# The mixer of a two-block transformer kernel turned round: q, k and v chunks last, linear attention and gating threaded through them, z tiles between the pairs, output products in two halves, head norms by token

## The reference

```
x = norm(ALPHA x + swiglu_half(x, w1, w3, w2))            # d_ff 2816
proj = x @ w_in                                            # 1024 -> u, v, qkv, z, beta, decay, cq, ck, cv, r, low
a = spatial_gating(u, v)                                   # mixes tokens in chunks of 128
b = gated_deltanet(silu(conv4(qkv)), z, beta, decay)       # 8 heads, chunks of 64, triangular solve, 8 steps
c = gla(cq, ck, cv, r, low)                                # 4 heads, linear attention in chunks of 64
x = norm(ALPHA x + [a b c] @ w_out)
x = norm(ALPHA x + swiglu_half(x, w1, w3, w2))
```

## Time and profile before

| what | us |
|---|---|
| median of three runs | 3182.92 |
| lowest and highest | 3181.77, 3183.39 |
| the profiled execution | 3187.82 |
| its span, first to last instruction | 3185.7 |
| PE busy | 2966.3 |
| DVE, ACT, POOL busy | 1318.6, 1110.5, 818.0 |

### The profile page before, as it was taken

One profiled execution on the slowest core, in us unless ns is written; L12 is line 12 of the kernel. 1 busy time (PEld: TensorE's weight loads), 2 busy tenths in 40 slices (PEclk: granted clock), 3 DMA queues, 4 the chain that ended last, 5 costly groups with the idle time before them and its releaser, 6 DMA issues.

```text
span 3185.7 us, 46789 instructions
## 1 busy us (share of the span) xinstructions
PE 2966.3 (93%) x19136; PEld 2399.5 (75%) x19136; DVE 1318.6 (41%) x1507; ACT 1110.5 (35%) x1290; POOL 818.0 (26%) x288
## 2 busy tenths in 40 slices
PE   7999999889999999988799999999999978899997
PEld 5776677658788887768678888788877858678886
DVE  3534444343223235636552323422157454643215
ACT  4334434422233325532233323333236421233323
POOL 4112211230101263334001135011443432000144
PEclk9999999979999999989999999999999989899998
DMA  4111111112222332210022233222332200122233
GB/s 167 40 60 53 43 45 46 53 53 93 94 92 92 111 140 88 93 54 1 15 79 93 92 119 135 81 104 92 125 126 84 84 28 1 41 80 95 103 125 113
DMA packets 36094, 257.50 MB, mean 81 GB/s; under 512 B 4032, under 2 KB 4080, under 8 KB 5872
## 3 DMA queue, kind: packets, MB, share of 16 engines
q1 hardware_dynamic: 34416, 249.65, 21.7%
q0 software_dynamic: 1536, 5.83, 0.6%
HBM read 253.30 MB, written 2.16 MB: 80 GB/s over the span
## 4 chain that ended last, share of the span: by engine, by line
PE 72%; issue 12%; DVE 6%; POOL 5%; ACT 3%; DMA 0%; ACTq 0%; DVEq 0%; POOLq 0%; SPq 0%
PE ps L2056 42%; PE ps L1572 6%; PE ps L1527 5%; PE ps L1564 4%; POOL wl L1194 4%; PE ps L2169 3%; PE ps L1627 2%; PE ps L1616 2%; PE ps L885 1%; ACT wh L1771 1%; PE ps L1582 1%; DVE wl L1882 1%; PE ps L1657 1%; DVE sqa L1915 1%; PE ps L2135 1%
## 5 line engine op out<-in xcount | busy, mean ns | idle before, releaser
L1194 POOL TENSOR_TENSOR wl<-raw,wh 128x2048 fp32r<-128x2048 f32 x114 | 525.2, 4607 | 817.7 <-ACT wh L1771 817.7
L2056 PE MATMUL ps<-xh,wh 128*128 128x512 f32 x1680 | 664.0, 395 | 20.7 <-DVE qkv L648 11.0
L2056 PE MATMUL ps<-xl,wh 128*128 128x512 f32 x1680 | 658.2, 392 | 0.0
L2056 PE MATMUL ps<-xh,wl 128*128 128x512 f32 x1680 | 658.0, 392 | 0.0
L1771 ACT ACTIVATE wh<-raw 128x2048 fp32r<-128x2048 f32 x224 | 427.5, 1908 | 408.1 <-PE ps L2056 351.9
L1882 DVE TENSOR_TENSOR wl<-raw,wh 128x2048 fp32r<-128x2048 f32 x112 | 285.7, 2551 | 578.8 <-ACT wh L1771 557.0
L2056 PEld LDWEIGHTS ps<-xh,wh 128*128 128x128 f32 x1680 | 317.7, 189 | 92.6 <-issue 14.7
L2056 PEld LDWEIGHTS ps<-xl,wh 128*128 128x128 f32 x1680 | 318.0, 189 | 67.8 <-issue 2.4
L2056 PEld LDWEIGHTS ps<-xh,wl 128*128 128x128 f32 x1680 | 317.8, 189 | 66.7
L1736 POOL TENSOR_TENSOR hl<-hf,hh 128x1024 f32 x44 | 105.8, 2404 | 980.8 <-ACT hh L1781 980.8
L2056 PE MATMUL ps<-hh,wh 128*128 128x512 f32 x704 | 277.1, 394 | 1.6 <-POOL wl L1194 1.2
(11 more groups left out here) (361 smaller groups left out, 4663.1 us busy)
## 6 DMA issues: line engine op xcount, KB each, us to landing
raw<-stream SPq DMA_DIRECT2D x232, 1024.0 KB, 4.8
btw<-bias_rows POOLq DMA_DIRECT2D x2, 1536.0 KB, 8.9
x<-x_in SPq DMA_DIRECT2D x1, 2048.0 KB, 8.2
out<-x SPq DMA_DIRECT2D x4, 512.0 KB, 2.6
sgp<-sg POOLq DMA_DIRECT2D x2, 640.0 KB, 4.0
cst<-consts SPq DMA_DIRECT2D x1, 1092.0 KB, 12.2
c<-bias_consts SPq DMA_DIRECT2D x1, 1024.0 KB, 15.7
bt<-bias_rows POOLq DMA_DIRECT2D x2, 512.0 KB, 9.2
```

Source lines behind the costliest of these rows:

```text
L1194: nc.gpsimd.tensor_tensor(wl[:, p, :], raw[:, p, :], wh[:, p, :].bitcast(F32), ALU.subtract).then_inc(s["chunk_lo"], 1)
L2056: mm = te.matmul(dst, wslice(w, k), r(k), start=(start and m == 0), stop=(stop and m == len(steps) - 1))
```

## The change

The input chunks come in another order: cq and ck, u, rows, cv, v, r, then the six of q, k and v, then the two of z. The chunks from q on are computed in quarters (`chunk_q`), and behind each quarter `between` puts small products: the decay columns behind the second quarter of chunk 6, the scores of the linear attention in chunk 7, its keys by token and the spatial gating in chunk 8, its states in chunk 9, its outputs in chunk 10. The four tiles of z stand one each between the pairs of the delta rule.

A head norm is now by token: four products with two columns give each token's mean squares (`norm_columns`, L542), ACT's root and DVE's reciprocal are taken of 16 or 32 columns, and eight products of 64x128 spread the result over the features (`norm_spread`, L551), which DVE multiplies from PSUM (L573). Squares stay on ACT.

The factors on keys and values move from DVE to POOL, by pairs, between the masks of the levels. Copies by token are by pairs too, and on ACT. The products that apply the inverse are emptied pair by pair, by ACT and DVE. Of the output, each tile's product is cut in two halves of four input tiles (0, 1, 6, 7 are known before the recurrence); the first halves of six tiles come ahead of any second half, and the last head norm stands between them. The weights of the output are stored in that order. Four products of 128x128 (`busy`) stand ahead of the wait before each layer norm and twelve behind it; nobody reads their result.

```diff
+OUT_K = ((0, 1, 6, 7), (2, 3, 4, 5))
+OUT_HALVES = ((0, 0), (0, 1), (0, 2), (0, 3), (0, 4), (0, 5), (1, 0), (1, 1), (1, 2), (1, 3), (0, 6), (0, 7), (1, 4), (1, 5), (1, 6), (1, 7))
+OUT_BANK = (4, 5, 6, 7, 0, 3, 1, 2)
...
+        IN_CQK, IN_AU, IN_ROWS, IN_CV, IN_AV, IN_CR, IN_QKV, IN_Z = 0, 1, 2, 3, 4, 5, 6, 12
...
+        def norm_columns(l, pe, g, tiles, bank, src):
+
+            for t in range(tiles):
+                pe.wait_ge(s["head_square"], l * NORMED + 2 * g + t + 1)
+                for m in range(4):
+                    c = 16 * g + 8 * t + 2 * m
+                    mm = nc.tensor.matmul(ps[:, bank, c:c + 2], tmp[:, src + t, m * P:(m + 1) * P], head_mean2, start=True, stop=True)
+            mm.then_inc(s["head_ms"], 1)
...
+        def norm_spread(l, pe, g, t, bank):
+
+            pe.wait_ge(s["head_rstd"], l * GROUPS + g + 1)
+            for m in range(4):
+                for b in range(2):
+                    c = 16 * g + 8 * t + 2 * m + b
+                    mm = nc.tensor.matmul(ps[64 * b:64 * b + 64, bank, m * P:(m + 1) * P], ncol[:, 1, c:c + 1].to_broadcast([P, 64]), C("ident"), start=True, stop=True)
+            mm.then_inc(s["head_spread"], 1)
...
+            if 0 <= g < 4 and q == 1:
+                norm_columns(l, pe, g, 2, 5, 4)
...
+            if at == (11, 2):
+                norm_columns(l, pe, 4, 2, 5, 4)
+            if 0 <= g < 4 and q in (3, 4):
+                t = q - 3
+                if g or t:
+                    pe.wait_ge(s["head_normed"], l * NORMED + 2 * g + t)
+                norm_spread(l, pe, g, t, 4)
...
+                    chunk_q(l, OFF_IN, j, j % 2, lambda q: between(l, pe, j, q))
+                between(l, pe, j, 4)
...
-        def heads_norm_pe(pe, n_tiles, n0, first=False):
-            for t in range(n_tiles):
-                n = n0 + t
-                pe.wait_ge(s["head_square"], n + 1)
-                if not first:
-                    pe.wait_ge(s["head_std"], n - 1)
-                nc.tensor.matmul(ps[:, 6 + t % 2, :], C("head_mean"), tmp[:, t % 2, :], start=True, stop=True).then_inc(s["head_ms"], 1)
...
-                nc.vector.reciprocal(tmp[:, 4 + t % 2, :], tmp[:, 2 + t % 2, :]).then_inc(s["head_rstd"], 1)
-                dve.wait_ge(s["head_rstd"], n + 1)
-                nc.vector.scalar_tensor_tensor(out=tiles[t], in0=tiles[t], scalar=factors[t], in1=tmp[:, 4 + t % 2, :],
-                                               op0=ALU.mult, op1=ALU.mult).then_inc(s["head_normed"], 1)
...
+            def z_tile(j, t):
+                if t == 0:
+                    pe.wait_ge(evac[j % 2], n_evac(l, j % 2, OFF_IN) + j // 2)
+                chunk_q(l, OFF_IN, j, j % 2, lambda q: between(l, pe, j, q), tiles=(t,))
+            z_tile(IN_Z, 0)
+            pair(0)
+            z_tile(IN_Z, 1)
+            pair(1)
+            pe.wait_ge(evac[1], n_evac(l, 1, OFF_IN) + IN_Z // 2)
+            turned(0)
+            z_tile(IN_Z + 1, 0)
+            pair(2)
...
+            for pr, ready in ((0, (s["pair_act"], l * 8 + 7)), (1, (s["pair_dve"], d0 + 3 * PAIR_DVE + 5)), (2, (s["pair_dve"], d0 + 3 * PAIR_DVE + 6)), (3, (s["pair_dve"], d0 + 3 * PAIR_DVE + 7))):
+                pe.wait_ge(*ready)
+                pe.sem_inc(s["apart_pe"], 1)
+                by_token(kT, pr, K_BANK[pr])
+            pe.wait_ge(s["by_token_sb"], l * 8 + 2)
+            turned(3)
...
+                if pr == 3:
+                    mix_rest(l, pool, ((0, au[:, 0, :]), (1, au[:, 1, :]), (6, cr[:, 0, :]), (7, cr[:, 1, :])), 0)
...
+            for lev in range(PAIRS):
+                masks(lev)
+                if lev == 0:
+                    pool.wait_ge(s["by_token_sb"], l * 8 + 8)
+                    pool.wait_ge(s["factor_dve"], l * 2 + 2)
+                    pool.wait_ge(s["factor_act"], l * 3 + 3)
+                gp.tensor_tensor(bk[:, lev], kN[:, lev], by_token(bgN, lev), ALU.mult).then_inc(s["factored"], 1)
+                gp.tensor_tensor(vN[:, lev], vN[:, lev], by_token(bN, lev), ALU.mult).then_inc(s["factored"], 1)
+                pool.wait_ge(s["factored"], l * 3 * PAIRS + 3 * lev + 2)
+                gp.tensor_tensor(kN[:, lev], kN[:, lev], by_token(kdN, lev), ALU.mult).then_inc(s["factored"], 1)
+            masks(PAIRS)
+            for j in (IN_Z, IN_Z + 1):
+                rest(pool, c_no(l, OFF_IN) + j + 2, j % 2)
...
-            ve.tensor_tensor(bk[:, :, :, :], kN[:, :, :, :], by_token(bgN), ALU.mult).then_inc(s["factor_dve"], 1)
-            dve.wait_ge(s["factor_act"], l * 3 + 3)
-            dve.wait_ge(s["factor_dve"], k0 + 3)
-            ve.tensor_tensor(kN[:, :, :, :], kN[:, :, :, :], by_token(kdN), ALU.mult).then_inc(s["factor_dve"], 1)
...
+                add_tiles((s["out_tile"], l * 3 + 2), 4, 1, s["out_early_x"])
+                dve.wait_ge(s["out_early_x"], l * 2 + 1)
+                add_sum(l, 1, 4, 6)
+                add_tiles((s["out_tile"], l * 3 + 2), 5, 1, evac[1])
+                dve.wait_ge(evac[1], n_evac(l, 1, OFF_OUT) + 1)
+                add_sum(l, 1, 5, 7)
...
+                rest_chunk(n_out + OUTP, 0)
+                add_tiles((s["out_tile"], l * 3 + 3), 6, 1, s["out_early_x"])
+                dve.wait_ge(s["out_early_x"], l * 2 + 2)
+                add_sum(l, 1, 6, 8)
+                add_squares(l, 1, (4, 5, 6))
...
+                    for kk in ks:
+                        k = OUT_K[h][kk]
+                        if n == OUT_HALVES.index((1, 0)):
+                            pe.wait_ge(s["mixed_lo"], l * 8 + 4 + kk + 1)
+                        c = 512 * i + P * kk
+                        for a, (w, r) in enumerate(((wh, xh), (wh, xl), (wl, xh))):
+                            mm = te.matmul(ps[:, OUT_BANK[t], :], w[:, m % 2, c:c + P], r[:, k, :], start=(h == 0 and kk == 0 and a == 0), stop=(h == 1 and kk == 3 and a == 2))
...
+                for n in (0, 1):
+                    out_half(n)
+                norm_columns(l, pe, 5, 4, 2, 1)
+                out_half(2)
+                for pr in range(PAIRS):
+                    if pr:
+                        pe.wait_ge(s["head_normed"], l * NORMED + 10 + pr)
+                    norm_spread(l, pe, 5, pr, 1)
...
+                out_half(11, (0, 1))
+                shift(l, 1)
+                out_half(11, (2, 3))
+                for n in (12, 13, 14):
+                    out_half(n)
+                out_half(15, (0, 1))
+                sums(l, 1)
+                out_half(15, (2, 3))
+                busy(4)
...
+            def busy(n):
+
+                for _ in range(n):
+                    te.matmul(shift_ps[:, 0:P], C("ident"), C("feat_mean"), start=True, stop=True)
```

743 lines of the change are left out of this document (412 added, 331 removed).

## The result

| | before | after | forecast |
|---|---|---|---|
| median, us (4 runs each) | 3183.15 (3181.77 to 3185.72) | 3128.85 (3125.57 to 3133.7) | 3113 (3082 to 3148) |
| ratio, 95% interval | | 0.983 (0.9813 to 0.9847) | |
| profiled execution, us (its span) | 3187.8 (3185.7) | 3125.6 (3123.7) | 3118.5 |

The account below looks back on a forecast made before the run. TensorE bounds the kernel by its work, idle gaps and half clock. Terms -24.8, -26.5, -5.4, -6.0 and -6.6 sum to -69.3 us: 3118.5 from the profiled 3187.8, median 3113; 8-in-10 range 3082 to 3148.

Parts of the forecast that it names:

- the likeliest case: Whole kernel: the sum of terms holds within its parts, 3098 to 3130 us; chance 0.52.
- the output stage: Recurrence to layer norm: 64.7 us instead of 67.7, -3.0 a layer, with a new wait and one clock drop.
- gap in chunk 11: Linear attention's sums by token wait for ACT's late squares: TensorE idles 1.9 us a layer.
- gap ahead of level one: End of the pairs: POOL's low parts and masks come late, together 3.6 us a layer.
- levels to end of recurrence, change: Copy of u becomes four operations, only the last, 0.7 us, exposed: -2.7 us a layer; POOL's factors cost nothing.
- wait at the sums: Output stage, before the sums of squares: DVE's list is late, TensorE waits about 6 us a layer.
- the pairs' broadcasts: Two broadcasts of a pair, parted: at most 0.85 us each instead of 1.06 for both, +1.6 for four pairs.
- the base of 207: TensorE's work before, first product to end of level one, without idle time and slow clock: some 207 us a layer.
- rival E: Head norms' ring of engine steps doesn't close within a chunk, q, k and v chunks wait, kernel slower; chance 0.04.
- Layer norms: Five norms: twelve `busy` products keep or raise the clock, 1 to 2.3 us each, -6.6 us in sum.
- B: More waits behind quarters and half clock at narrow norm products than found: +32, 3145 us (3130 to 3172); chance 0.2.
- D: POOL's factor operations make it the bound of the levels: +4 us a layer, 3121 us, inside the likeliest case's range.

Follow-up runs that it names:

- a load like that of the wide reciprocals: Changed kernel with two unused 512-column reciprocals on VectorE ahead of each short reciprocal of q's and k's norms: 3145.1 us, ratio 0.9867 to before.
- the factors: Changed kernel with the twelve factor operations back on VectorE, ahead of its level updates: 3151.6 us, ratio 0.9884 to before.
- the experiment on low parts: Changed kernel with two of four low parts at the pairs' end made by VectorE instead of GpSimd: 3127.5 us, ratio 0.981 to before.
- the joined kernel: Changed kernel with five edits: fewer `busy`, low parts on VectorE, pair 3's mask later, VectorE's output-stage order, chunk 11's sums one quarter later: 3103.5 us, ratio 0.9733.
- the second trace of the changed one: Trace from rerunning the changed kernel unaltered beside the experiments: 3131.5 us, ratio 0.9814 to before; the trace's span is 3129.6 us.

## Why the prediction was right

The mechanism held in its main line: in the input stage and the mixer TensorE had been waiting for other engines, with its clock down, and work threaded behind quarters and halves costs TensorE time but removes both. How the 45 to 51 us part between the threading, the narrow norms and the output in halves isn't shown: only a load like that of the wide reciprocals (14 to 17 us), the factors (20 to 22) and `busy` were taken singly. That the time came out within the likeliest case is in part luck, as the work and the output stage show. Point by point, a layer:

| | forecast | layer 0 | layer 1 |
|---|---|---|---|
| first product to end of level one | 231.3 | 232.9 | 232.5 |
| third chunk, chunk behind the half one | 1.2, 1.1 | 1.45, 0.41 | 1.45, 0.41 |
| gap in chunk 11 | 1.9 | 1.46 | 1.46 |
| gap ahead of level one | 3.6 | 3.58 | 3.57 |
| levels to end of recurrence, change | -2.7 | -0.7 | -1.8 |
| output stage | 64.7 | 64.8 | 64.9 |
| wait at the sums | 6 | 4.74 | 4.73 |

**Work.** 232.9 less gaps of 6.9 and 3 for two spells of half clock leaves 223 where 220.3 stood. The norms cost less than taken: the narrow sums of two tiles start 1.70 us ahead of what follows, a spreading 1.03, so 1.88 a tile instead of 2.04, +10.3 for ten. The scores cost 0.62 each half, 1.24 instead of the forecast 1.7. The prediction's estimate by the Trainium skill ("TensorE: Matmul & The Clock Gate", "Why this matters for your kernels"), products in distinct row groups side by side, was 1.8; the rows contradict that estimate. A mis-sized term is the pairs' broadcasts, "at most 0.85 each":

```profile
1385.72 1.12 PE L915 MATMUL ps<-gam,cst 8*128 8x512 f32 x2
1386.77 1.15 PE L921 MATMUL ps<-qkv 64*64 64x64 f32 x32
1387.85 1.12 PE L927 MATMUL ps<-gam,cst 8*128 8x512 f32 x2
```

Parted, each takes 1.05 to the next start, as long as the two together before: +4.2 for four pairs, not +1.6. In sum +14.8 instead of +13.4. The 0.2 us of a threaded group was in no term. In this stretch PE goes from long products to a small group at 25 places, and at 7 in the kernel before: 18 more, an estimate of 3.6 us. It was made up for by a slip in the base of 207: thirteen and a half chunks at the prices given there (10.8 each, two of them 11.7) are 147.6 us and not 152. The two errors, of some 4 us each, nearly cancelled, and only so was the work right to 2.7 us.

**Gaps and clock in the stretch.** Right to 0.7 us each. GpSimd's list as the cause of the gap ahead of level one is shown by the experiment on low parts; that the squares are late in chunk 11 by the row's releaser and by the joined kernel, where sums one quarter later have no wait. The reserve of the ring, named as the way to lose it all (rival E), measured 3.4 us for q and k and 2.0 for the linear attention.

**Levels and recurrence.** The wait of 2.7 us on the copy of u is gone, as forecast. But PE's "issue" gaps from level one's end to the recurrence's are 2.8 us in layer 0 and 2.6 in layer 1, against 0.8 and 1.3 before: one to two us given back to the fetching of code, for which the prediction had no term. GpSimd's factors cost nothing in the levels; no mask releases PE in levels two to four. What they save is larger than the stretch of before showed.

**Output stage.** Right in sum, by luck. The terms that the prediction names (43.5, 3.9, 4.0, 1.0, 6 and 2) make 60.4 us and not 64.7. Some 3 of the missing 4.3 are the layer norm's sums ahead of the end (two of 1.05 us at full clock) and the first `busy` products (1.05), which it doesn't name. Two further errors nearly cancel: the wait is 1.3 us shorter, the clock costs 3.8 us instead of 2 (the two sums 1.9 each for 1.05, six products 2.7 for 1.4, `busy` 1.9 for 1.0).

**Layer norms.** -6.6 in sum was forecast. Outside the two stretches the rows give -0.7 (which lies ahead of the first norm's last sums), -4.3, +3.5, -0.2 and -3.8: -5.5. The +3.5 at the loop's end is the step that failed: the prediction gave all five norms the same gain, though PE idles 5.44 us at that one in the trace of before and 2.98 at the first. There the instruction packet sets the time, and the twelve products bring one more.

**The sum.** The profiled execution came out 7.1 us above the sum: 2.8 in the two stretches, 2.9 in the levels and recurrences, 0.3 in the output stages, 1.1 at the norms. Two of the norms' gains, 2.2 and 1.6 us of full clock in the first two chunks, lay inside the stretch, where a spell-free start was already counted: part of the -6.6 was counted twice. The other 8.2 us to the median aren't a fault of the sum: the profiled execution of before lay 4.9 us above its median, that of after 3.3 below.

**The rivals.** B's waits behind quarters and spells at each group of narrow sums didn't come in the stretch; single spells at the head norm's group did in the output stage, in the joined kernel and in the second trace of the changed one. D is refuted in the levels.

## What to carry to other kernels

Where another engine's steps stand in a ring with TensorE, thread them between quarters or halves of solid products, and make wide operations in the ring narrow: a place costs 0.2 us, a wait costs its length and often a spell at half clock. Count the places, before and after. Order an engine's list by who waits: 2.3 us of work for a later stage, put ahead of a sum, cost more here than any arithmetic. Filler products can keep the clock through a gap, but ahead of this loop's jump twelve of them put the next stage off by 3.2 us, one instruction packet more. Where PE idles for "issue", look at the instruction queue of the DMA.
